# A hybrid decoder step on one core: first product pair of each MLP, last down steps, norm tails and first HGRN2 weights reordered

## What is computed

```python
def rmsnorm(x, g):
    xf = x.astype(jnp.float32)
    y = xf * lax.rsqrt(jnp.mean(xf * xf, -1, keepdims=True) + EPS)
    return (y * g.astype(jnp.float32)).astype(x.dtype)
...
        x = x + mix.astype(dt)
        h = rmsnorm(x, p['norm_mlp'][layer])
        x = x + (jnp.square(jax.nn.relu(h @ p['mlp_up'][layer])) @ p['mlp_down'][layer]).astype(dt)
    y = rmsnorm(x, p['norm_final'])
```

## Time and profile before

| | us |
|---|---|
| median of 3 runs | 3350.61 |
| the profiled execution | 3352.3 |
| its span, first to last instruction | 3350.2 |
| TensorE busy with matmuls | 3192.0 (95%) |
| VectorE busy | 2122.2 (63%) |
| GpSimd busy | 1279.1 (38%) |
| ScalarE busy | 1165.8 (35%) |
| mean granted TensorE clock | 0.977 of full speed |

### The profile page before, as it was taken

One profiled execution on the slowest core, in us unless ns is written; L12 is line 12 of the kernel. 1 busy time (PEld: TensorE's weight loads), 2 busy tenths in 40 slices (PEclk: granted clock), 3 DMA queues, 4 the chain that ended last, 5 costly groups with the idle time before them and its releaser, 6 DMA issues. The chain is left out here.

```text
span 3350.2 us, 74980 instructions
## 1 busy us (share of the span) xinstructions
PE 3192.0 (95%) x31716; PEld 3017.6 (90%) x31716; DVE 2122.2 (63%) x2892; ACT 1165.8 (35%) x2373; POOL 1279.1 (38%) x760
## 2 busy tenths in 40 slices
PE   8999889999999988999999989999998999999997
PEld 7999768888887888999999989999998899999997
DVE  5112874664665748666777784566546966667776
ACT  3344122332332334444333342221222444443333
POOL 3322120110113025444677733222211544457783
PEclk9999899999999999999999989999999999999998
DMA  5113630100011102444544411111112144454442
GB/s 170 59 58 109 190 118 9 33 30 16 30 36 48 67 30 74 142 143 143 201 147 146 131 46 57 66 63 59 59 60 112 58 137 145 143 199 144 144 146 82
DMA packets 151199, 322.70 MB, mean 96 GB/s; under 512 B 16904, under 2 KB 50356, under 8 KB 150744
## 3 DMA queue, kind: packets, MB, share of 16 engines
q1 hardware_dynamic: 106480, 242.53, 22.3%
q10 hardware_dynamic: 44392, 75.42, 6.6%
HBM read 227.12 MB, written 93.12 MB: 96 GB/s over the span
## 5 line engine op out<-in xcount | busy, mean ns | idle before, releaser
L247 PE MATMUL psum<-act_hi,w_hi 128*128 128x352 f32 x2088 | 704.7, 337 | 21.2 <-DVE act_lo L4169 5.7
L232 POOL TENSOR_TENSOR w_hi<-w_raw,derived 128x1024 fp32r<-128x1024 f32 x87 | 169.4, 1947 | 1415.6 <-PE psum L247 1339.3
L247 PE MATMUL psum<-act_hi,w_lo 128*128 128x352 f32 x2088 | 677.7, 325 | 0.0
L247 PE MATMUL psum<-act_lo,w_hi 128*128 128x352 f32 x2088 | 676.6, 324 | 0.0
L247 PEld LDWEIGHTS psum<-act_hi,w_hi 128*128 128x128 f32 x2088 | 397.1, 190 | 49.8 <-issue 15.2
L247 PEld LDWEIGHTS psum<-act_lo,w_hi 128*128 128x128 f32 x2088 | 398.7, 191 | 2.5 <-issue 0.2
L247 PEld LDWEIGHTS psum<-act_hi,w_lo 128*128 128x128 f32 x2088 | 397.9, 191 | 0.0
L1072 PE MATMUL psum<-ff_near,ff_w_hi 128*128 128x264 f32 x2048 | 382.7, 287 | 8.9 <-ACT ff_a L1202 5.9
L1072 PEld LDWEIGHTS psum<-ff_near,ff_w_hi 128*128 128x128 f32 x2048 | 320.0, 190 | 15.5 <-issue 15.1
L1072 PE MATMUL psum<-ff_far,ff_w_hi 128*128 128x264 f32 x1536 | 285.9, 287 | 12.3 <-DVE ff_r L1407 6.2
L1072 PE MATMUL psum<-ff_near,ff_w_lo 128*128 128x264 f32 x1024 | 292.7, 286 | 0.0
(11 more groups left out here) (556 smaller groups left out, 7496.5 us busy)
## 6 DMA issues: line engine op xcount, KB each, us to landing
ff_du_raw<-u SPq DMA_DIRECT2D x224, 264.0 KB, 2.8
w_raw<-weights SPq DMA_DIRECT2D x87, 512.0 KB, 3.3
u<-ff_stage SPq DMA_DIRECT2D x128, 264.0 KB, 2.2
ff_raw<-mlp SPq DMA_DIRECT2D x64, 512.0 KB, 3.9
u<-ff_side SPq DMA_DIRECT2D x96, 264.0 KB, 3.7
s_cache<-cache_a ACTq DMA_DIRECT2D x32, 512.0 KB, 6.8
ff_dt<-mlp SPq DMA_DIRECT2D x64, 256.0 KB, 4.4
ff_dt<-mlp SPq DMA_DIRECT2D x32, 512.0 KB, 7.1
```

The source lines that it names most:

```text
L232: pool.tensor_tensor(hi, raw, self.zeros, ALU.add).then_inc(s.sem, s.step())
L247: last = pe.matmul(out, w[:, k, :], h[:, k, cols], start=(start and k == ks[0] and m == 0), stop=(stop and k == ks[-1] and m == 2))
```

## The change

All line numbers in the fences marked as diffs are those of the kernel before. Both MLPs get the same edits; the C weights concern the first MLP alone.

1. *Entry of the up half.* For the first pair the low parts of the weight blocks 5, 3 and 4 go from GpSimd to VectorE; GpSimd waits for the last low part of T4 before it starts on the second pair. The last square (`sq_last`) is no longer added on VectorE: TensorE adds it by three more matmuls with ones. The quadrants of the first pair are taken in the order 22, 12, 11, 21, and the weight sums of the second pair stand behind 11.
2. *From up to down.* ScalarE keeps b ahead of a square in the last pair. The low parts of U of step 1 stand ahead of step 0's additions, and `mixed_last` of the last pair stands inside step 0.
3. *The last steps.* U of step 27 has places of its own, so its low parts are made during step 25; ScalarE makes the weights of step 26 in one go.
4. *Norm tails.* Another order of squares; the final norm takes the sums of squares between the F units as the middle norm does, its first sum over TensorE stands behind F8 in place of F9.
5. *C weights.* The first four are loaded to four buffers during the last steps; ScalarE makes their high parts right behind step 27's U, GpSimd only the low parts.

```diff
@@ class MiddleNorm(Norm)
-    SQUARES = (0, 1, 2, 3, 8, 9, 10, 11, 4, 16, 5, 17, 6, 18, 7, 19, 12, 13, 14, 15, 20, 21, 22, 23)
+    SQUARES = (0, 1, 2, 3, 8, 9, 10, 11, 16, 17, 18, 19, 4, 5, 6, 7, 12, 13, 14, 15, 20, 21, 22, 23)
+    SUMS = {1: (1,), 2: (2, 3), 3: (9, 10), 4: (11, 17), 5: (18, 4), 6: (19, 5), 7: (6,), 8: (7,)}
...
         self.act_root(act, 0)
+        act.wait_ge(self.K.plan.steps["pool"].sem, self.weights)
         for t in range(4):
+            self.act_square(act, 12 + t)
             self.act_high(act, t)
-            self.act_square(act, 12 + t)
+        act.wait_ge(*self.K.plan.at(self.last_unit))
@@ class FinalNorm
-        for t in {0: (1,), 1: (2,), 2: (3,), 5: (4,), 6: (5,), 7: (6,), 8: (7,), 9: (9,), 10: (10, 11, 12), 11: (13,),
-                  12: (14, 15), 13: (17, 18, 19)}.get(u, ()):
+        more = {9: (12,), 10: (13,), 11: (14,), 12: (15,), 13: (20,), 14: (21,), 15: (22, 23)}
+        for t in (*self.SUMS.get(u, ()), *more.get(u, ())):
             self.dve_sum(dve, t)
-        for t in {12: (0,), 13: (1,), 14: (2, 3), 15: range(4, 8)}.get(u, ()):
-            self.dve_scale(dve, t)
+        if 10 <= u < 15:
+            self.dve_scale(dve, u - 10)
         if u == 15:
-            for t in range(20, 24):
-                self.dve_sum(dve, t)
-            for t in range(8, 24):
+            for t in range(5, 24):
                 self.dve_scale(dve, t)
...
-        if u == 9:
+        if u == 8:
             self.pe_sum(pe, 0)
@@ class MLP
+    def low_label(self, w, p):
+        return f"{'dve' if w == 0 and p in (5, 3, 4) else 'split'}.{self.n}.{w}.low{p}"
...
         for p in (1, 2, 6, 7):
             self.weight_low(pool, 0, p)
-        for p in (5, 3, 4):
-            self.weight_low(pool, 0, p)
+        pool.wait_ge(*at(f"dve.{n}.lo_T4_1"))
...
-        pe.wait_ge(*at(f"dve.{n}.acc{KC - 1}"))
+        pe.wait_ge(*at(f"dve.{n}.acc{KC - 2}"))
+        pe.wait_ge(*at(f"act.{n}.sq{KC - 1}"))
...
+            pe.matmul(out, K.ones[:, :], self.rstd[:, cols], start=True, stop=False)
+            pe.matmul(out, K.ones[:, :], self.sq_last[:, cols], start=False, stop=True).then_inc(s.sem, s.step(f"pe.{n}.sum{c}"))
@@ def act
         keep_both(w, 0)
         self.w_high(act, 0, 0)
-        self.square_out(act, w, "11")
         self.w_high(act, 0, 1)
         keep_both(w, 1)
+        self.square_out(act, w, "11")
...
-        for q in range(2):
-            self.w_high(act, self.STEPS - 1, q)
         for q in range(self.WIDTH):
-            self.u_high(act, self.STEPS - 1, q)
-            if q >= 2:
-                self.w_high(act, self.STEPS - 1, q)
+            self.w_high(act, end, q)
+        for q in range(2):
+            self.w_high(act, last, q)
+        for q in range(self.WIDTH):
+            self.u_high(act, end, q)
+        for q in range(2, 4):
+            self.w_high(act, last, q)
+        for q in range(self.WIDTH):
+            self.u_high(act, last, q)
+        if self.following is not None:
+            self.following.act_weights(act)
@@ def dve
         self.mixed_out(dve, w)
-        self.mixed_last(dve, w)
+        for q in range(self.WIDTH):
+            self.u_lower(dve, 1, q)
         for step in range(self.STEPS - 2):
             for j, d in enumerate(self.UNITS):
                 self.down_add(dve, step, d)
-                if j < 2:
-                    for q in (2 * j, 2 * j + 1):
+                if step == 0 and j == 2:
+                    self.mixed_last(dve, w)
+                for q in (2 * j % 4, 2 * j % 4 + 1):
+                    if 0 < step and j < 2:
                         self.u_lower(dve, step + 1, q)
+                    elif step == self.STEPS - 3:
+                        self.u_lower(dve, step + 2, q)
@@ class MixC
+    def act_weights(self, act):
+        s = self.K.plan.steps["act"]
+        act.wait_ge(self.K.sem("w_loaded"), 16 * (self.w0 + 4))
+        for n in range(4):
+            for label in self.first_free[n]:
+                act.wait_ge(*self.K.plan.at(label))
+            act.activation(flat(self.K.slots[self.slot(0, n)][0]), self.first_raw[n][:, :], ACT.Copy)\
+                .then_inc(s.sem, s.step(f"act.C.weight{n}"))
...
+        for n in range(4):
+            hi, lo = (flat(t) for t in self.K.slots[self.slot(0, n)])
+            pool.wait_ge(*K.plan.at(f"act.C.weight{n}"))
+            pool.tensor_tensor(lo, self.first_raw[n][:, :], hi.bitcast(F32), ALU.subtract).then_inc(s.sem, s.step() + s.step())
```

160 lines of the change are left out of this document (94 added, 66 removed).

## The result

| | before | after |
|---|---|---|
| median, us | 3353.02 (7 runs) | 3321.41 (7 runs) |
| the profiled execution: span, us | 3350.2 | 3311.4 |
| ratio | | 0.9898, 95% interval 0.9879 to 0.9918 |

The account below looks back on a forecast made before the run. TensorE was busy 95% of the span, so gains lay only in its waits and the half clock behind them. Terms 20 + 6.5 + 7.5 + 7.2 = 41.2 us off 3352.3 gave 3311 us, range 3297 to 3331.

Parts of the forecast that it names:

- Entry: Start of the up half, both MLPs: TensorE's waits in the first pair go, 10 us each, 20 for both.
- so of the 10.5 us nearly all goes: Entry of the up half: nearly all of the 10.5 us lost in the 32 us window goes, less 0.5.
- signs that I named as "wrong": Waits of 3 us or more at P4 or the second pair's P1, among the signs that would refute the forecast.
- the count of 255: Entry, sign of being right: some 255 matmuls in the 32 us from P5 on.
- The first rival: VectorE becomes the bound at the entry: half of the 20 us lost, passage gains nothing, 3327; chance 0.20.
- Both come from one thing: Entry: waits of 1.78 us (block 5) and 3.12 us (P4) both come from GpSimd low parts beside VectorE's chain.
- Up to down: Passage from up to down half, both MLPs: L1 fills idle time, wait moves to step 2; 6.5 us for both.
- The bound of 15: Upper bound for the passage from up to down: 15 us if the column sums shorten too.
- First MLP to C: Passage from first MLP to C: wait for L27 stays, wait ahead of the sum goes; 7.5 us.
- the third rival: At C: a VectorE run keeps the ports, L27 meets no C low part, sum some 5 us better.
- the second of its list: Rival that the ports stay with VectorE: L27 not held up, passage gains its full 6.4; 3298, chance 0.13.
- Last steps and final norm: End of second MLP and final norm: 5.6 us go, new wait of 1.1, tail gains 2.7; 7.2 us.

Follow-up runs that it names:

- the second profile: The kernel after, unchanged, run again beside a combined kernel as its yardstick: 3321.91 us (6 runs), ratio 0.9901 to the kernel before.

## Why the prediction came out as it did

**Entry, 20 us forecast, 9.5 measured (8.6 in the second profile): the step that failed.** The total came out within the range although this term was twice too large, since others were too small. The first pair is right in each of its times. P5 was to begin some 15.8 us behind the MLP's first matmul and began at 16.0; P4 was to start at 21.8 and started at 22.3 with a wait of 0.30 us; the second pair began 5.8 us earlier. What failed is "so of the 10.5 us nearly all goes". The 32 us window held the second pair as well, and in it a wait of 2.33 us for a copy by ScalarE with some 1.5 us lost at half clock behind it, for which the working had no term. TensorE of before, ahead of P6 of the second pair:

```profile
1324.10 0.48 PE L1072 MATMUL psum<-ff_near,ff_w_hi 128*128 128x264 f32 x2 [2.33 <-ACT ff_a L1202]
```

I asked of the second pair only when its first low part comes. After the change TensorE reaches it 5.8 us earlier and meets VectorE and ScalarE where they were: 3.39 us at P5, with half clock behind it. The signs that I named as "wrong", P4 and the second pair's P1, were clean; the stop is at its P5, where I did not look, and the count of 255 was not met. With the copies of b and c moved the entries won 7.5 and 6.9 us in place of 4.8 and 4.7. The first rival had the size of this term right (half of the 20 us) and the cause in part: VectorE is late, and the copies of b and c behind its results and behind a load turn that into TensorE's wait. It had the place wrong (P4 and P6), and its price for the passage, nothing, too.

**"Both come from one thing"** held for one of the two. The wait of 1.78 us ahead of P5 was for the low part of 7.53 us of the earlier trace rows, as its row says, and that was so long because of VectorE's run beside it. For the wait ahead of P4 the order of quadrants counts: with no GpSimd work beside VectorE's chain, but the old order, TensorE still waited 1.69 and 1.84 us. P4 began 26.6 us behind the MLP's first matmul before and 22.3 after; with the old order alone it was 23.8, with the low parts on GpSimd alone 22.7. Its row names a quadrant; I had explained away the name by the next long row.

**Up to down, 6.5 forecast, 9.8 and 7.5 measured.** L1 filled the idle time and the wait moved to step 2 as forecast; it was 1.7 us, not some 4.5. L2.3 was to be ready at 1661 to 1662 and TensorE there at 1656; 9.3 us had been won ahead, which makes them 1652 and 1647. TensorE was there (it waits from 1647.0 on), but the last L2 was ready at 1646.27 + 2.88 = 1649.15. The mis-sized terms are on VectorE: the column sums took 5.17 us, not 6.86, and with L1 out of step 0 the rest came some 1 us sooner too. The bound of 15 had named shorter column sums, and I did not take it. With the moves undone they took 6.85 us again; by what way the moves shorten them is not tested.

**First MLP to C, 7.5 forecast, 9.6 and 10.2 measured.** C's low parts began at 1929.08, where 1942.6 less the 14 us won ahead is 1928.6; L27 took 2.64 and 2.21 us each; L27.3 was ready at 1940.5 where 1955 less 14 is 1941; from F0 to the sum it took 20.2 us where it had taken 27.3, 7.1 less. The rest of the gain lies behind the sum, where before ran at half clock after a wait of 7.03 us. (What the prediction calls "the third rival" there is the second of its list.) None of the kernels has the old making of C's weights back, so this gain is read from the rows and not shown by an undoing. In kernels that do not differ here the stretch took 34.0 to 37.3 us, so the size is known to some 3 us, and why it varies stays open. Some of it may be given back: the 657 us behind it were 0.3 to 3.2 us longer in all changed kernels than in the one profile of before, which I can't tell from the variation of that stretch (656.8 to 660.0 over all profiles).

**Last steps and final norm, 7.2 forecast, 7.2 measured.** The wait of F4 went, the new one was 1.03 us for 1.1 forecast, VectorE had 11.0 us behind the last matmul (3297.5 to 3308.51). Only the place of the first sum was undone in a kernel of its own; that U27's places and the order of squares make the rest was not tested apart.

**The sum.** 41.2 us forecast in the touched places; 36.0 in one profile and 33.4 in the other. The entry was 10.5 too high, the passage and C together 5.4 too low. That the first profile showed a span 38.8 us shorter is the luck of the first 1280 us; the ratio, 34 us, is the fairer number.

## What to carry to other kernels

A window's loss has to be split by waits before an edit is credited with it: list every wait in the window, name the one that each edit takes away, and price what is left as a loss that stays. A wait that goes brings TensorE to the next one earlier, so read on (here through two more pairs), and on each engine in that stretch ask what stands ahead of the copy that frees the bank. Delaying work on a shared path may only move the conflict along, as C's low parts did. And when two edits remove the same wait, undoing either alone shows nothing of it: compare where the operand lands and when the engine gets there.

## What the runs showed of the hardware

A VectorE instruction with both inputs in SBUF and a GpSimd low part slow each other down, as if they took turns: 1.63 to 1.80 us for V1 to V4 and 1.75 for each low part beside them, against 0.70 and 1.28 alone. One of VectorE's inputs in PSUM, and it keeps its time beside the same low parts: 0.69 us in the row at 1317.73. The Trainium skill ("SBUF — State Buffer", section "Who interferes with whom") states that a VectorE instruction with two inputs in SBUF contends with a GpSimd instruction that reads SBUF, and that one with at most one such input does not, outside certain faster modes of VectorE; the traces agree. Not explained by turns is the run of scaled subtractions, beside which one low part of GpSimd took 7.53 and 6.38 us while VectorE stayed at 0.70 us each. In both kernels the low part ended 1.1 us behind the end of that run, as if the run held the path throughout; no run here took that apart.

The same program's first 1280 us, with no edit in them, varied by 14 us over 14 profiles. Effects under that are to be read from stretches with the same work, not from the span of one profile.
